# Sigmoid gates made with tanh, and gelu moved behind the attention, in a two-block network on one core

## The reference

```
h = rms_norm(x, norm1_w);  z = h @ w_in          # columns: u, q, k, v, gs, ga
# state-space mixer: y from u by a complex linear scan (sines and cosines of the angles)
y = gelu(y);               y_ssm  = y * sigmoid(y @ w_glu + b_glu)
# differential attention: 8 heads of two maps, softmax each, p0 - lam * p1, times v, rms_norm per head
y_attn = diff_attention(z[q], z[k], z[v], ...)
m = sigmoid(z[gs]) * (y_ssm @ w_proj_ssm) + sigmoid(z[ga]) * (y_attn @ w_proj_attn)
x = x + m @ w_out          # then rms_norm, and (silu(h @ Wg) * (h @ Wu)) @ Wd
```

## Time and profile before

| | us |
|---|---|
| median of three runs | 2384.34 |
| lowest and highest | 2382.87, 2385.12 |
| the profiled execution | 2388.75 |
| its span, first to last instruction | 2387.0 |
| mean granted clock of PE, of full | 0.993 |
| busy: PE, DVE, ACT, POOL | 2329.6, 1475.6, 1174.3, 177.0 |

### The profile page before, as it was taken

One profiled execution on the slowest core, in us unless ns is written; L12 is line 12 of the kernel. 1 busy time (PEld: TensorE's weight loads), 2 busy tenths in 40 slices (PEclk: granted clock), 3 DMA queues, 4 the chain that ended last, 5 costly groups with the idle time before them and its releaser, 6 DMA issues.

```text
span 2387.0 us, 35950 instructions
## 1 busy us (share of the span) xinstructions
PE 2329.6 (98%) x14891; PEld 1943.3 (81%) x14891; DVE 1475.6 (62%) x1854; ACT 1174.3 (49%) x1651; POOL 177.0 (7%) x188
## 2 busy tenths in 40 slices
PE   8999989999999999999999999999999999999998
PEld 8777767888888888888888898878888888888886
DVE  5999956755554554454444456746765558466666
ACT  5676656644454444444344344534563546335643
POOL 5000000002000000000000001120000010301043
PEclk9999999999999999999999999999999999999999
DMA  9544564565666666666666676434546665336576
GB/s 255 174 155 152 164 195 151 160 199 180 186 192 187 185 191 188 189 190 187 192 190 190 192 225 180 127 95 130 162 128 222 191 188 150 99 106 161 142 217 197
DMA packets 306116, 415.61 MB, mean 174 GB/s; under 512 B 53577, under 2 KB 164745, under 8 KB 305185
## 3 DMA queue, kind: packets, MB, share of 16 engines
q1 hardware_dynamic: 300128, 395.63, 56.2%
q0 software_dynamic: 5504, 17.60, 2.3%
q10 hardware_dynamic: 320, 0.08, 0.0%
HBM read 406.94 MB, written 7.87 MB: 174 GB/s over the span
## 4 chain that ended last, share of the span: by engine, by line
PE 82%; DVE 9%; ACT 3%; DMA 2%; issue 2%; POOL 1%; ACTq 0%; SPq 0%; DVEq 0%; POOLq 0%
PE banks L643 80%; DVE wp_hl L1239 3%; ACT wp_hl L1972 2%; DMA first_rows<-ln_b 1%; POOL xr L2616 1%; PE banks L763 1%; POOL xr L2614 0%; DVE r_SA L1794 0%; PE banks L775 0%; ACT L1972 0%; DMA xt<-x 0%; DVE u_z L1586 0%; DVE nsd L1649 0%; DMA lng<-ln_g 0%; PE banks L892 0%
## 5 line engine op out<-in xcount | busy, mean ns | idle before, releaser
L1239 DVE TENSOR_TENSOR wp_hl<-raw,wp_hl 128x1024 fp32r<-128x1024 f32 x740 | 912.5, 1239 | 824.4 <-ACT wp_hl L1972 823.6
L1972 ACT ACTIVATE wp_hl<-raw 128x1024 fp32r<-128x1024 f32 x740 | 782.3, 1060 | 1029.4 <-PE banks L643 1003.9
L643 PE MATMUL banks<-wp_hl,XX_hl 128*128 128x512 f32 x3840 | 897.2, 393 | 6.4 <-DVE wp_hl L1239 6.1
L643 PEld LDWEIGHTS banks<-wp_hl,XX_hl 128*128 128x128 f32 x3840 | 716.3, 188 | 167.9 <-issue 11.0
L643 PE MATMUL banks<-XX_hl,wp_hl 128*128 128x256 f32 (+1 forms) x3584 | 634.4, 332 | 6.4 <-DVE wp_hl L1239 5.2
L643 PEld LDWEIGHTS banks<-XX_hl,wp_hl 128*128 128x128 f32 x3584 | 528.4, 191 | 77.2 <-issue 14.9
L643 PE MATMUL banks<-wp_hl,FF_hl 128*128 128x512 f32 x1056 | 240.7, 389 | 0.0
L643 PEld LDWEIGHTS banks<-wp_hl,FF_hl 128*128 128x128 f32 x1056 | 197.9, 188 | 41.0
L643 PE MATMUL banks<-wp_hl,MXa_hl 128*128 128x512 f32 x384 | 88.6, 389 | 1.3 <-DVE wp_hl L1239 1.3
L643 PE MATMUL banks<-wp_hl,MM_hl 128*128 128x512 f32 x384 | 88.4, 390 | 0.0
L643 PEld LDWEIGHTS banks<-wp_hl,MXa_hl 128*128 128x128 f32 x384 | 72.0, 188 | 16.6 <-DVE wp_hl L1239 1.7
(11 more groups left out here) (467 smaller groups left out, 1794.6 us busy)
## 6 DMA issues: line engine op xcount, KB each, us to landing
raw<-w_in SPq DMA_DIRECT2D x304, 512.0 KB, 3.9
raw<-w_out SPq DMA_DIRECT2D x96, 512.0 KB, 4.6
raw<-w_ffn_gate SPq DMA_DIRECT2D x88, 512.0 KB, 3.7
raw<-w_ffn_up SPq DMA_DIRECT2D x88, 512.0 KB, 3.7
raw<-w_ffn_down SPq DMA_DIRECT2D x88, 512.0 KB, 3.9
raw<-w_proj_attn SPq DMA_DIRECT2D x16, 512.0 KB, 5.0
raw<-w_proj_ssm SPq DMA_DIRECT2D x16, 512.0 KB, 3.9
raw<-w_glu SPq DMA_DIRECT2D x8, 512.0 KB, 4.5
```

The source lines that it names most:

```text
L643: return e.matmul(o, lhsT, rhs, start=start, stop=stop, skip_group_check=True)
L1239: return tt(d, src, hi, SUB)
L1972: return e.activation(o, x, func, bias=bias, scale=scale)
```

## The change

Sigmoid of the gates becomes (1 + tanh(x / 2)) / 2. ACT computes tanh with a halved scale (`rs[:, 6:8]`, made once on DVE, and a halved `b_glu`); DVE's product with the gate adds 1 in the same instruction; the half is taken where the result is rounded and split. ACT gets three explicit table loads: silu's ahead of the first sine, silu's again after the root of the q and k norms, and exp's after the q and k blocks. Gelu leaves its place ahead of the attention: it stands behind the attention's turns in two halves, and the four splits into YP follow it, on ACT and DVE. The `Pace` calls of PE and POOL stay.

```
@@ -496,7 +496,7 @@
     def over(name):
         return s_mm, OF[name].over
 
-    XQ, XS, XA, XD = marks("x_sq", "q"), marks("x_sum", "s"), marks("x_root", "s"), marks("x_diag", "r", "d")
+    XQ, XS, XA, XD = marks("x_sq", "q"), marks("x_sum", "s"), marks("x_root", "s"), marks("x_diag", "r", "h", "d")
     XRP, XR = marks("x_row_t", "p"), marks("x_row", "r")
     XTR, NH, NL, LY = marks("x_turn", "t"), marks("x_hi", "h"), marks("x_lo", "l"), marks("ln_y", "y")
     LNS, LNR, LX, YT = marks("ln_stat", "b"), marks("ln_mv", "m", "r"), marks("ln_x", "x"), marks("y_tok", "m", "b")
@@ -1317,14 +1317,15 @@
                 for i in range(2):
                     m = 2 * c + i
                     e.wait_ge(s_evA, j.freed[i][1])
-                    tt(sig[i], sig[i], pair(yT, m), MUL).then_inc(GV.made("g", m), 1)
+                    stt(out=sig[i], in0=sig[i], scalar=1.0, in1=pair(yT, m), op0=ADD, op1=MUL).then_inc(GV.made("g", m), 1)
                     e.wait_ge(*GA("h", m))
-                    lo(XX.lo(512 * m, 512 * m + 512), v2(sig[i]), XX.hi_f(512 * m, 512 * m + 512)).then_inc(YSL.made("l", m), 1)
+                    stt(out=XX.lo(512 * m, 512 * m + 512), in0=v2(sig[i]), scalar=0.5, in1=XX.hi_f(512 * m, 512 * m + 512),
+                        op0=MUL, op1=SUB).then_inc(YSL.made("l", m), 1)
             elif n in ("pa", "ps"):
                 c = int(l)
                 g = sga[:, 4 * c:4 * c + 4, :] if n == "pa" else sgs(c)
                 for i in range(2):
-                    tt(pair(g, i), pair(g, i), b[i], MUL).then_inc(s_evV, 1)
+                    stt(out=pair(g, i), in0=pair(g, i), scalar=1.0, in1=b[i], op0=ADD, op1=MUL).then_inc(s_evV, 1)
             elif n in ("wo", "fd"):
                 c = int(l)
                 for i in range(2):
@@ -1409,6 +1410,7 @@
             e.reciprocal(rs[:, 2:4], rs[:, 2:4]).then_inc(XD.made("r", stage), 1)
             e.wait_ge(*XD("r", stage))
             if stage == 0:
+                ts(rs[:, 6:8], rs[:, 2:4], 0.5, None, MUL).then_inc(XD.made("h", stage), 1)
                 for t in range(2):
                     last = ts(dg[:, 128 * t:128 * t + 128], ident, rs[:, 2 + t:3 + t], None, MUL)
                 last.then_inc(XD.made("d", stage), 1)
@@ -1445,6 +1447,7 @@
         e.wait_ge(*PCV("c2"))
         ts(col("qw"), col("qw"), 0.125, None, MUL)
         ts(col("subln"), col("subln"), 0.8, None, MUL)
+        ts(pcol[:, PC["bglu"]:PC["bglu"] + 8], pcol[:, PC["bglu"]:PC["bglu"] + 8], 0.5, None, MUL)
         for l in range(2):
             a = PC[f"mu{l}"]
             last = ts(omu[:, 16 * l:16 * l + 13], pcol[:, a:a + 13], -1.0, 1.0, MUL, ADD)
@@ -1649,12 +1652,12 @@
                     e.reciprocal(sd, sd).then_inc(ONV.made("r", p), 1)
                     e.wait_ge(*ONV("r", p))
                     stt(out=pair(aT, p), in0=pair(aT, p), scalar=col("subln"), in1=sd, op0=MUL, op1=MUL).then_inc(ONV.made("o", p), 1)
-                if u == 3 and what != "S":
-                    i = 2 * (what == "O") + c
-                    e.wait_ge(*YSA("h", i))
-                    lo(YP.lo(512 * i, 512 * i + 512), pair(yT, i), YP.hi_f(512 * i, 512 * i + 512)).then_inc(YSV.made("l", i), 1)
                 main(at.share(2.9))
-        main(at.go(10))
+        main(at.go(4))
+        for i in range(4):
+            main(at.go(2))
+            e.wait_ge(*YSA("h", i))
+            lo(YP.lo(512 * i, 512 * i + 512), pair(yT, i), YP.hi_f(512 * i, 512 * i + 512)).then_inc(YSV.made("l", i), 1)
         main(at.until("ga3"))
         for i in range(4):
             e.wait_ge(*ASA("h", i))
@@ -1668,7 +1671,8 @@
             main(at.go(6))
             for m in (2 * c, 2 * c + 1):
                 e.wait_ge(*MSA("h", m))
-                lo(MM.lo(512 * m, 512 * m + 512), B[4 + m % 4], MM.hi_f(512 * m, 512 * m + 512)).then_inc(MSV.made("l", m), 1)
+                stt(out=MM.lo(512 * m, 512 * m + 512), in0=B[4 + m % 4], scalar=0.5, in1=MM.hi_f(512 * m, 512 * m + 512),
+                    op0=MUL, op1=SUB).then_inc(MSV.made("l", m), 1)
         for c in range(4):
             main(at.until(f"wo{c}"))
             if c == 3:
@@ -2067,20 +2071,20 @@
                 c = int(n[2])
                 act(vM2[:, 0, 512 * c:512 * c + 512], b[0], ACT.Copy).then_inc(s_evA, 1)
             elif n in ("gs", "ga"):
-                e.wait_ge(*XD("r"))
+                e.wait_ge(*XD("h"))
                 for i in range(2):
                     d = pair(sgs(int(l)), i) if n == "gs" else pair(sga, 2 * int(l) + i)
-                    act(d, b[i], ACT.Sigmoid, scale=rs[:, 2 + i:3 + i]).then_inc(s_evA, 1)
+                    act(d, b[i], ACT.Tanh, scale=rs[:, 6 + i:7 + i]).then_inc(s_evA, 1)
             elif n == "glu":
                 c = int(l)
                 for i in range(2):
                     m = 2 * c + i
                     if c:
                         e.wait_ge(*YSL("l", m - 2))
-                    act(sig[i][:, 0:256], b[i][:, 0:256], ACT.Sigmoid, bias=col("bglu", 2 * m))
-                    act(sig[i][:, 256:512], b[i][:, 256:512], ACT.Sigmoid, bias=col("bglu", 2 * m + 1)).then_inc(s_evA, 1)
+                    act(sig[i][:, 0:256], b[i][:, 0:256], ACT.Tanh, bias=col("bglu", 2 * m), scale=0.5)
+                    act(sig[i][:, 256:512], b[i][:, 256:512], ACT.Tanh, bias=col("bglu", 2 * m + 1), scale=0.5).then_inc(s_evA, 1)
                     e.wait_ge(*GV("g", m))
-                    hi(XX.hi(512 * m, 512 * m + 512), v2(sig[i])).then_inc(GA.made("h", m), 1)
+                    act(XX.hi(512 * m, 512 * m + 512), v2(sig[i]), ACT.Copy, scale=0.5).then_inc(GA.made("h", m), 1)
             elif n == "wo":
                 c = int(l)
                 for i in range(2):
@@ -2165,6 +2169,7 @@
         e.wait_ge(*DL("l2"))
         act(lamc[:, 2:4], lamc[:, 0:2], ACT.Exp).then_inc(DLA.made("e"), 1)
         main(at.share(1.95))
+        e.preload_act_table(ACT.Silu)
         e.wait_ge(*SV("f5"))
         act(fa, f, ACT.Abs).then_inc(SA.made("fa"), 1)
         act(sn, f, ACT.Sin, scale=TWOPI)
@@ -2229,8 +2235,7 @@
             main(at.share(1.75))
             e.wait_ge(*DB("t", m))
             act(qk_block(m), B[4 + m % 4], ACT.Identity, scale=col("qw" if m < 4 else "kw")).then_inc(DC.made("c", m), 1)
-        e.wait_ge(*YV("y", 7))
-        act(flat(yT), flat(yT), ACT.Gelu_apprx_tanh).then_inc(GEL.made("g"), 1)
+        e.preload_act_table(ACT.Exp)
 
         def d_scores(c, u):
             k = 2 * u + c
@@ -2259,12 +2264,16 @@
                     p = 2 * u + c
                     e.wait_ge(*ONP("n", p))
                     act(nrm[c][1], B[4 + c], ACT.Sqrt, bias=K["eps5"], scale=1.0 / 128).then_inc(OSD.made("s", p), 1)
-                if u == 3 and what != "S":
-                    i = 2 * (what == "O") + c
-                    e.wait_ge(*GEL("g"))
-                    hi(YP.hi(512 * i, 512 * i + 512), pair(yT, i)).then_inc(YSA.made("h", i), 1)
                 main(at.share(2.9))
-        main(at.go(10))
+        e.wait_ge(*YV("y", 7))
+        for i in range(2):
+            w = slice(4 * i, 4 * i + 4)
+            act(flat(yT[:, w, :]), flat(yT[:, w, :]), ACT.Gelu_apprx_tanh).then_inc(GEL.made("g", i), 1)
+            main(at.go(2))
+        for i in range(4):
+            e.wait_ge(*GEL("g", i // 2))
+            hi(YP.hi(512 * i, 512 * i + 512), pair(yT, i)).then_inc(YSA.made("h", i), 1)
+            main(at.go(2))
         main(at.until("ga3"))
         for i in range(4):
             e.wait_ge(*ONV("o", i))
@@ -2277,7 +2286,7 @@
             main(at.go(6))
             for m in (2 * c, 2 * c + 1):
                 e.wait_ge(*MTN("t", m))
-                hi(MM.hi(512 * m, 512 * m + 512), B[4 + m % 4]).then_inc(MSA.made("h", m), 1)
+                act(MM.hi(512 * m, 512 * m + 512), B[4 + m % 4], ACT.Copy, scale=0.5).then_inc(MSA.made("h", m), 1)
         for c in range(4):
             main(at.until(f"wo{c}"))
             if c == 3:
```

## The result

The changed kernel takes 2392.85 us in the median of 7 runs (2390.78 to 2394.79), the kernel before 2385.61 in 7 runs beside them (2382.87 to 2388.98). The ratio is 1.0029 with a 95% interval of 1.0019 to 1.004: slower by 7.2 us at the medians. The forecast was 2392.7, which was +8.35 on the median known then.

What follows compares the result with a forecast made beforehand. The prediction took PE to bound the kernel, busy 2329.6 of 2387.0 us. Gap +8.45, clock +2.7 and gain -2.8 made +8.35 us on the median 2384.34, so 2392.7, range 2388.5 to 2396.0.

Steps and rivals of the forecast that it cites:

- No steps left for the portions: At the attention's end: no matmul steps remain between gelu's moved portions, so all moved work lies bare before glu0.
- The rival that the portions are covered: At the attention's end: matmul steps still cover the moved work, only the 2.8 us gain is left, 2381.5 us; chance 0.05.
- The gap: Between ga3 and the product that reads YP: PE starts 8.45 us later, bounds 7.2 to 9.2.
- The clock: Behind the gap: PE's granted clock falls to 1.2 GHz, costing 2.7 us, between 0 and 4.
- the rival of no fall: Behind the gap: the clock does not fall, +5.65 us, 2390.0 us; chance 0.04.
- The three places: In the attention: PE waits at the first pair, gs3's gate and a weight piece shrink by 0.98, 0.43 and 1.4 us.
- the doubled gain: Gaps from 300 to 412: ACT's freedom also speeds weight splits, twice the gain, +5.5 us, 2389.9 us; chance 0.05.
- the end of all waits: Attention from 300 to 412: all PE waits, some 9 us, go; +2 us, 2386.3 us; chance 0.04.
- Tanh in exp's table: Gates among the exps: exp's table also serves tanh, so eight of 16 loads go; rival, outside exp's set, 0.08.
- Gate and gelu on one table: In the gap: one table load serves ga3's gate and gelu, 1.28 us less, 2391.4 us; chance 0.08.
- The rest at nothing: Elsewhere: gates, fused forms, output gate's load, small DVE instructions and earlier sine table together cost nothing.
- The sum: Whole kernel: +8.45 + 2.7 - 2.8 = +8.35 us, median 2392.7 us; forecast's chance 0.66.

Runs made afterwards that it cites:

- the run that keeps PE busy: The changed kernel plus 64 matmuls on PE, result unread, between ga3 and the output gate's product; 2389.06 us, ratio 1.0018 against the kernel before.
- the move alone: The kernel before, sigmoid gates kept, with only gelu and its splits moved behind the attention's turns and exp's table loaded ahead; 2396.15 us, ratio 1.005.
- early fetch: The changed kernel with gelu's table loaded right after the attention's last root, ahead of ga3's gate; 2389.66 us, ratio 1.0022 against the kernel before.

## Why the prediction held, step by step

**No steps left for the portions.** Right. No matmul stands between ga3 and the product, and moving the same work into the last pair's turns, where steps are left, takes the whole loss away. The rival that the portions are covered falls.

**The gap.** 8.45 forecast, from the product's old start to its new one; 8.70 measured so (the 8.55 of the timeline is PE's idle time alone). Each instruction was in its place: two loads, gate, gelu in two halves, one rounding, one remainder. DVE's timeline has that remainder by itself:

```profile
457.23 0.69 DVE L1239 TENSOR_TENSOR YP_hl<-uT,YP_hl 128x512 fp32r<-128x512 f32 x1 [2.77 <-ACT YP_hl L1976]
```

Up to its end, 457.92, the sum is right to 0.02 us. What it lacks is the 0.26 us from there to the product's first matmul at 458.18, which it put at nothing. Taking 2.56 us of loads out took 2.85 off, putting the second half of gelu (0.95) behind the first roundings took 0.81 off.

**The clock.** The mechanism was right, shown by the run that keeps PE busy; the size was off. I took 2.7 from one stretch of 6.4 us at the low level; it cost 1.72 in the changed kernel, and over the four kernels with the fall 1.52 to 2.24 (the upper in the move alone, where 22.43 and 3.13 make 25.56, less 23.32). The share was right: of 4.0 us of the product at the low level 1.72 are lost, the 43% of the sum. The length was wrong: the four products ran at the low level for 3.5 to 4.8 us by the windows view, not for 6.4, and in the changed kernel the level had been low for 6 us of the gap already, while PE had nothing to do. "An idle of 8 us will not do better than one of 3" did not hold against the earlier trace rows. In the changed kernel even the stretch of the earlier trace rows is shorter: the level is up again by 73, where before it was still low in 74 to 75. PE's timeline and the windows view of the changed kernel there:

```profile
68.31 1.13 PE L643 MATMUL banks<-uT,BT 32*128 32x256 f32 x8 [2.85 <-DVE uT L1304]
```

```profile
73.00:74.00 1.00, 1.00 (x5) 0.78 (x5) 0.97 (x2) 0.00 (x0) 0.00 (x0) 0.95 0.00 0
```

The same idle of 2.85 us, the same work behind it: eight matmuls took 1.13 us here and 2.08 in the earlier trace rows. One row for this cost was too few; the rival of no fall is out, but my figure lay at the dear end of what executions show. The Trainium skill, TensorE: Matmul & The Clock Gate, section "What's actually happening", says that the number of matmuls at the low level varies from run to run with the same program. These rows are of two programs and only fit it. The changed kernel's own seven executions differ too, from 0.991 to 0.993 in mean granted clock.

**The three places.** 2.8 forecast, 2.73 measured: 0.98 for 0.98, 0.45 for 0.43, 1.30 for 1.4. The first hangs on gelu's move and the third on the gates, as forecast; the second, which the prediction put down to a load and a gate, comes with either half alone. Neither the doubled gain nor the end of all waits came: the others stand where they stood.

**Tanh in exp's table.** Right. No gate among the exps carries a load any more, and eight loads are left as counted. The rule of the Trainium skill, ScalarE: Activation LUTs, section "Table sets: the hidden batching unit", that exp and tanh share a set, is borne out by this count.

**Gate and gelu on one table.** The rival of 0.08 did not come in the changed kernel, where each has its load. The early fetch showed that one table can serve both, so it was the program's choice of tables that kept them apart, not the tables.

**The rest at nothing.** The start moved by -0.3, where I had set the two small VectorE instructions against the earlier sine table at zero. It lies within the scatter of single executions: the row at 68.31 stands at 68.33, 68.06, 67.49, 68.03 and 68.49 in the five experiments with the same start, and at 67.44 in the move alone, which has the start of before. That the fused forms and the output gate's tanh cost nothing is borne out by the run without the move: with all of them in, it is not slower than before.

**The sum.** +8.35 forecast, +7.4 by the terms, +7.2 at the medians: 1.0 of the difference to the terms is the clock, 0.3 the start, less 0.3 for the gap and the three places. That 2392.7 came within 0.2 us of 2392.85 is luck: the change cost 1.1 us less than forecast, and the kernel before was 1.3 us slower beside it than in the three runs known then. The forecast for the profiled execution, 2397.1, was 6.3 us too high for the one that was profiled; the offset between one execution and the median is several us in this kernel and goes either way, so only the difference carries over.

## What to carry to other kernels

Before moving work "behind" a stage and spacing it out, count the steps of the bounding engine that are left there; a spacer that has reached its cap returns nothing, and the work lies bare. Price a bare gap by walking the queue of the engine that fills it, instruction by instruction, and add the clock's fall as a range from several stretches, not from one. A saving on an engine that does not bound pays only where a wait of the bounding engine ends on it: of 10 us of loads that went and 1.9 of gelu that left the attention, 2.7 were seen there.

## What the runs showed of the hardware

- After nearly the same idle of 2.8 to 2.9 us and with the same work behind it, PE's clock was low until about 75 in the execution of before and until about 73 in the changed one, and the first eight matmuls ran at either level: over the eight profiled executions, with idle times of 2.84 to 2.92 us, they took 1.13 us in four and 2.08 in four. A wait of 2.6 us was followed by a fall in one kernel's execution and by none in another's.
- The low clock of the gap outlasted it by some 4 us (3.5 to 4.8 in four kernels), into the product; with matmuls in the gap, even such as nobody reads, the clock stayed at 2.4 GHz.
- One table load, fetched for gelu's tanh form, served tanh as well: the load at 446.91 in the early fetch, the gate at 449.84 and gelu at 450.98.
- The second block's same 24 matmuls, behind the same wait of 1.0 us, took 5.14 us in one execution and 3.11 in another.
